# Attention gates from eight 32-column float32 products, with the tangent taken after the turn

## The reference, cut to what matters

```
h = rms_norm(x, norm1_g)
z = h @ w_in                       # 512 x 1024 by 1024 x D_IN
z_sc, z_q, z_kv, z_ng, z_ret, z_pool, z_gate = split(z)
g = sigmoid(z_ng.reshape(B, S, G, J, 3))          # the gates: 24 numbers for each position
o = g[..., 0:1] * o_cmp + g[..., 1:2] * o_slc + g[..., 2:3] * o_win
```

## Time and profile before

| what | value |
| --- | --- |
| median of 3 runs | 2067.34 us (2065.33 to 2068.14) |
| the profiled execution | 2065.34 us |
| its span, first to last instruction | 2063.5 us |
| PE busy, share of the span | 2034.1 us, 99% |
| DVE, ACT, POOL busy | 1188.9 us, 682.6 us, 916.8 us |
| mean granted PE clock | 0.996 of full speed |

### The profile page before, as it was taken

How to read it: one execution, slowest core, us unless ns; L and a number is a source line. 1 busy time by engine, 2 the same in 40 slices (tenths; PEclk the granted TensorE clock), 3 DMA queues, 4 the chain that set the end, 5 groups by cost and what they waited for, 6 DMA issues and landing times.

```text
span 2063.5 us, 31457 instructions
## 1 busy us (share of the span) xinstructions
PE 2034.1 (99%) x9836; PEld 1639.1 (79%) x9836; DVE 1188.9 (58%) x1717; ACT 682.6 (33%) x1011; POOL 916.8 (44%) x672
## 2 busy tenths in 40 slices
PE   9999999999999999999999999999999999999997
PEld 7777767888888888888887777678888888888886
DVE  7777766332327788862258667572222378888522
ACT  5365333332322222222234553333323232222222
POOL 4422333445445555555544223344444455555553
PEclk9999999999999999999999999999999999999998
DMA  5311222222223223223233113223222223222233
GB/s 211 108 52 43 77 87 88 94 100 93 98 94 102 92 92 102 92 95 112 95 126 95 53 42 96 84 82 102 92 99 94 96 87 102 93 100 97 99 104 109
DMA packets 57429, 194.87 MB, mean 94 GB/s; under 512 B 7040, under 2 KB 7552, under 8 KB 57216
## 3 DMA queue, kind: packets, MB, share of 16 engines
q1 hardware_dynamic: 52576, 186.17, 27.0%
q10 hardware_dynamic: 4768, 7.61, 1.4%
HBM read 186.67 MB, written 2.10 MB: 91 GB/s over the span
## 4 chain that ended last, share of the span: by engine, by line
PE 93%; DVE 4%; ACT 1%; issue 1%; DMA 0%; SPq 0%; DVEq 0%; ACTq 0%
PE acc L1220 28%; PE acc L1222 28%; PE acc L1221 28%; PE o L1435 2%; PE s L1405 2%; PE t L1416 2%; PE o L1475 1%; PE s L1465 1%; PE s L1313 0%; DVE pool_early L1064 0%; DMA w_raw<-weights_dram 0%; DVE sc L1058 0%; PE s L1491 0%; PE t L1456 0%; ACT pr L569 0%
## 5 line engine op out<-in xcount | busy, mean ns | idle before, releaser
L435 POOL TENSOR_TENSOR w_lo<-w_raw,w_hi 128x512 fp32r<-128x512 f32 x668 | 916.6, 1394 | 1123.2 <-ACT w_hi L457 1107.7
L1220 PE MATMUL acc<-xg_hi,w_hi 128*128 128x512 f32 x1904 | 768.7, 404 | 5.9 <-DVE sc L740 2.1
L1222 PE MATMUL acc<-xg_hi,w_lo 128*128 128x512 f32 x1904 | 743.3, 390 | 0.0
L1221 PE MATMUL acc<-xg_lo,w_hi 128*128 128x512 f32 x1904 | 742.6, 390 | 0.0
L457 ACT ACTIVATE w_hi<-w_raw 128x1024 fp32r<-128x1024 f32 x336 | 355.4, 1058 | 813.0 <-PE acc L1222 785.0
L1220 PEld LDWEIGHTS acc<-xg_hi,w_hi 128*128 128x128 f32 x1904 | 357.9, 188 | 113.8 <-issue 37.7
L1221 PEld LDWEIGHTS acc<-xg_lo,w_hi 128*128 128x128 f32 x1904 | 358.2, 188 | 77.0 <-issue 6.4
L1222 PEld LDWEIGHTS acc<-xg_hi,w_lo 128*128 128x128 f32 x1904 | 357.8, 188 | 76.2
L1097 DVE TENSOR_TENSOR work<-acc,rstd 128x512 f32<-128x512 f32 x64 | 44.1, 690 | 256.2 <-PE acc L1222 256.2
L1220 PE MATMUL acc<-act_hi,w_hi 128*128 128x512 f32 x352 | 136.9, 389 | 0.0
L1221 PE MATMUL acc<-act_lo,w_hi 128*128 128x512 f32 x352 | 136.9, 389 | 0.0
(11 more groups left out here) (208 smaller groups left out, 2206.6 us busy)
## 6 DMA issues: line engine op xcount, KB each, us to landing
w_raw<-weights_dram SPq DMA_DIRECT2D x339, 512.0 KB, 3.3
x<-xT_dram SPq DMA_DIRECT2D x8, 256.0 KB, 5.5
rot<-rq ACTq DMA_DIRECT2D x16, 128.0 KB
rot<-rk ACTq DMA_DIRECT2D x16, 128.0 KB
dec<-decay_dram ACTq DMA_DIRECT2D x8, 256.0 KB, 3.6
out_dram<-x SPq DMA_DIRECT2D x8, 256.0 KB, 2.6
con<-consts_dram SPq DMA_DIRECT2D x1, 1406.0 KB, 10.5
w1k<-w_dram SPq DMA_DIRECT2D x2, 512.0 KB, 8.7
```

Of the source, the lines that this page charges most:

```text
L435: nc.gpsimd.tensor_tensor(w_lo[:, slot, part], w_raw[:, slot, part], w_hi[:, slot, part].bitcast(F32), ALU.subtract).then_inc(lo_ready, 1)
L1220: mm(tile, w_h, right_hi, start=first, stop=False)
L1221: mm(tile, w_h, right_lo, start=False, stop=False)
L1222: return mm(tile, w_l, right_hi, start=False, stop=last)
```

## The change

The gate tile is no longer made of the split weights and the split, scaled input. DVE adds `w_hi` and `w_lo` of the 32 columns that matter back to one float32 matrix and multiplies it by the gain `norm1` (`gate_w`, 128 x 8 x 32, two instructions). PE then makes eight plain float32 matmuls of 32 weight columns with `x` itself: chunks 0 to 3 go to column groups 0 to 3 (partitions 0 to 31, 32 to 63 and so on of the bank), chunks 4 to 7 to the same four again. The bank so holds four partial sums. `take(10)` is as before. The turn is now four float32 matmuls with `fold`, a 128x32 matrix of four stacked identities, which sums the four parts while it turns. `fold` is made anew in each layer by a reduction of `ident` on DVE, ahead of `take(10)`. ACT takes the tangent from the turned bank (128x96) in SIDE's slot 2, and DVE ends the sigmoid in place. The loading and splitting of groups 10 and 11 stay.

```diff
+        gate_w = at("gate_w", [P, CH, 32], F32, R)
+        fold = small[:, 0:32]
...
-                    if g == 11:
-                        act.wait_ge(acc_free, 1 + L * TILES + 12)
-                        nc.scalar.activation(sc[:, 2, :], sc[:, 2, :], ACT.Tanh, scale=0.5).then_inc(a_made, 1)
...
+                            if e[0] == "gate":
+                                act.wait_ge(s_done, s_use(L, e))
+                                nc.scalar.activation(gates[:, :, :], s_of(e)[:, :].rearrange("p (k n) -> p k n", k=QT)[:, :, 0:3 * HEADS],
+                                                     ACT.Tanh, scale=0.5).then_inc(a_made, 1)
...
                 s_end(ins, "vc")
+                g = A_TILES.index("gate")
+                dve.wait_ge(lo_ready, 1 + 2 * (L * GROUPS + (g + 1)))
+                halves_of = [w[:, g % RING, :].rearrange("p (c n) -> p c n", c=CH)[:, :, 0:32].bitcast(F32) for w in (w_hi, w_lo)]
+                then(ve.tensor_tensor(gate_w[:, :, :], halves_of[0], halves_of[1], ALU.add))
+                v_end(ve.tensor_tensor(gate_w[:, :, :], gate_w[:, :, :], V("norm1", 0, DC).unsqueeze(2).to_broadcast([P, DC, 32]), ALU.mult), "gate_w")
                 take(9, qT[:, 3, :])
...
                 then(ve.tensor_tensor(kc[:, 0:NCMP], kc[:, 0:NCMP], C("cos_c", NCMP), ALU.mult))
+                then(ve.tensor_reduce(fold, ident.rearrange("p (j i) -> p i j", j=4), AX.X, ALU.add))
                 take(10, sc[:, 2, :])
...
                 def gate(e):
-                    s_wait(e)
-                    s_end(ve.tensor_scalar(gates[:, :, :], s_of(e)[:, :].rearrange("p (k n) -> p k n", k=QT)[:, :, 0:3 * HEADS],
-                                           1.0, 0.5, ALU.add, ALU.mult), e, wait=True)
+                    dve.wait_ge(a_made, a_count(L, "gate"))
+                    s_end(ve.tensor_scalar(gates[:, :, :], gates[:, :, :], 1.0, 0.5, ALU.add, ALU.mult), e, wait=True)
...
+                    if name == "gate":
+                        pe.wait_ge(v_made, v_count(L, "gate_w"))
+                        alone(pe)
+                        for c in range(DC):
+                            rows = slice(32 * (c % 4), 32 * (c % 4) + 32)
+                            ins = mm(acc[g % 2][rows, :], gate_w[:, c, :], x[:, c, :], start=c < 4, stop=c >= 4)
+                        ins.then_inc(halves, 4)
...
                 def gate(e):
-                    pe.wait_ge(a_made, a_count(L, "gate"))
+                    pe.wait_ge(acc_free, 1 + L * TILES + 12)
                     b = s_begin(e)
-                    alone(pe)
+                    last_wait()
                     for k in range(QT):
-                        ins = nc.tensor.transpose(b[:, k * P:k * P + 32], sc[0:32, 2, k * P:(k + 1) * P], ident[0:32, 0:32])
+                        ins = mm(b[:, k * P:k * P + 32], sc[:, 2, k * P:(k + 1) * P], fold, start=True, stop=True)
```

More of the change, by code:

```diff
@@ L149 @@
 assert len(S_USES) % 2 == 0 and len(T_USES) % 2 == 0
-V_MADE = ["win_k", "k0_scaled", "k1_scaled", "win_v", "k0", "k1", "arg", "hid", "q0", "q1", "q2", "q3", "kc", "center"]
+V_MADE = ["win_k", "k0_scaled", "k1_scaled", "win_v", "k0", "k1", "arg", "hid", "q0", "q1", "gate_w", "q2", "q3", "kc", "center"]
 A_MADE = ["hid", "gate"]
@@ L557, in _ @@
                         for e in SIDE[n]:
-                            if e[0] == "cmp_scores":
+                            if e[0] == "gate":
+                                act.wait_ge(s_done, s_use(L, e))
+                                nc.scalar.activation(gates[:, :, :], s_of(e)[:, :].rearrange("p (k n) -> p k n", k=QT)[:, :, 0:3 * HEADS],
+                                                     ACT.Tanh, scale=0.5).then_inc(a_made, 1)
+                            elif e[0] == "cmp_scores":
                                 act.wait_ge(v_made, v_count(L, e))
@@ L1247, in tile_free, with quarter @@
                     pe.wait_ge(acc_free, 1 + v)
-                def quarter(g, q, tile, wait=False, loop=None, per=0, done=1):
+                def quarter(g, q, tile, wait=False, loop=None, per=0):
                     if q == 2:
@@ L1257, in quarter, with projection @@
                     if q % 2:
-                        ins.then_inc(halves, done if q == 3 else 1)
-                def projection(g, tile, wait=False, norm=None, loop=None, per=0, done=1):
+                        ins.then_inc(halves, 1)
+                def projection(g, tile, wait=False, norm=None, loop=None, per=0):
                     for q in range(4):
-                        quarter(g, q, tile, wait, loop, per, done)
+                        quarter(g, q, tile, wait, loop, per)
                         if norm and q == norm[2]:
@@ L1326, in _ @@
                 for g, name in enumerate(A_TILES):
+                    if name not in ("gate", "pad"):
+                        group_here(g)
                     if name != "pad":
-                        group_here(g)
                         tile_free(g)
-                    if name != "pad":
+                    if name == "gate":
[5 more added lines that the diff above has]
+                        ins.then_inc(halves, 4)
+                    elif name != "pad":
                         projection(g, acc[g % 2], wait=1 if g == 0 else False,
                                    norm=("sumsq1", L * 16 + DC, 3, sum_squares) if g == 2 else
-                                   ("spread1", L * 2 + 1, 1, spread_root) if g == 3 else None,
-                                   done=3 if A_TILES[g + 1] == "pad" else 1)
+                                   ("spread1", L * 2 + 1, 1, spread_root) if g == 3 else None)
                     if g == 6:
@@ L1581, in _ @@
             ins.then_inc(spread_ready, 1)
-CHAIN_LAYER, CHAIN_J, CHAIN_F, CHAIN_D = 165, 4, 15, 2
+CHAIN_LAYER, CHAIN_J, CHAIN_F, CHAIN_D = 167, 4, 15, 2
 def _constants():
```

## The result

| | before | changed |
|---|---|---|
| median of 8 runs each | 2067.64 us | 2075.06 us (2070.67 to 2077.53) |
| profiled execution, span | 2065.34, 2063.5 us | 2077.08, 2075.3 us |
| mean granted clock over the span | 0.996 | 0.991 |

The changed kernel takes 1.0035 times as long (95% interval 1.0026 to 1.0044). It is slower, by 7.4 us; the forecast was 5.6 us, 2072.9 us. Eight products took the place of 24, PE has less to do, and the kernel lost time. The eight runs of the changed kernel differ in their clock: the fastest, 2070.67 us, has a mean granted clock of 0.994, the slowest, 2077.53 us, one of 0.990.

A forecast was written before the change was run, and what follows sets the result against it. PE held 93% of the chain of waits, but DVE's path to `take(10)` set the floor. Late start 1.35, clock 1.4 and turn 0.3 us, twice, less 0.5, made 5.6 us: 2072.9 us, range 2067.0 to 2077.5.

The forecast's parts named there:

- rival A: The forecast: DVE's chain to `take(10)` ends last, the clock falls in both layers; 2072.9 us (2070.5 to 2076), chance 0.46.
- F: PE's saving is kept: `take(10)` follows the gate products, group 12 starts 2.9 us early; 2062.1 us, chance 0.06.
- E: The gate products' column groups don't overlap, group 12 starts 1.7 us late; 2071.0 us, chance 0.07.
- B: Same DVE chain, but the clock stays, or falls while PE stands still anyway; 2070.1 us, chance 0.22.
- rival C: More DVE steps, the reduction too, stand behind POOL, and the clock costs its full 1.7 us; 2075.8 us, chance 0.11.
- Term 1: PE's gate products: 24 matmuls of some 5.4 us become eight taking 2.0 us, saving 3.4 us in each layer.
- Term 2: DVE's two new instructions ahead of `take(9)`: 0.9 us with the gap, `take(9)` 0.6 us late (0.5 to 0.8).
- Term 3: DVE's rotation of q2: two instructions stand behind POOL's halves, the next runs free; the delay stays 0.6 us.
- Term 4: POOL's group 13 starts earlier, so DVE's small keys' step L876 waits about 1.1 us (nothing to 1.27).
- Term 5: The `fold` reduction on DVE ahead of `take(10)`: 0.3 us, upper end 1.1 us more.
- Term 6: PE's clock falls to half behind a 5.1 us stop before group 12: 1.4 us, bounds 0 and 2.1.
- Term 7: The gates' turn on PE with the narrower moving side: 0.3 us more, bounds -0.1 and 0.45.

The follow-up runs named there:

- PE's part alone: The changed kernel without DVE's three new instructions, gate products taking columns of x as weights (gates not the reference's): 2074.10 us, ratio 1.0032.
- the first kernel with an early take: The changed kernel with gate weights by ACT, `fold` made early, `take(10)` right behind `take(9)`, attention steps four slots later: 2068.02 us, ratio 0.9995.
- DVE's part alone: The kernel before plus DVE's three new instructions in their places, results unused: 2068.56 us, ratio 1.0009.
- the control with 24 products: The kernel before with its 24 gate products into the idle bank `t_bank[1]` and later slots for turn and attention: 2065.24 us, ratio 0.9989.

## Why the prediction was right, point by point

- **The mechanism** (rival A): right. DVE's chain sets `take(10)`, and everything that PE saved turned into waiting. The kernel with PE's part alone and those that take the wait away show it from both sides. F, the saving kept, needed `take(10)` out of its place, as the prediction said. E is refuted by the span of 1.92 us, B by the 5.80 us of work at the half clock, D by the step of 1.24 us. By its number alone rival C, 2075.8 us, lies nearer to the measured 2075.06 than A's 2072.9. It took two things more than A: the reduction behind POOL, which did not happen (0.37 us), and a larger price of the clock, which did. So the rows decide for A's chain, and the clock's price was nearer to C's and above that too.
- **Term 1**: 2.0 us forecast, 1.92 measured. The 5.4 us of the 24 products stand, though the subtraction given for them, 5.69 less 0.46, is 5.2: 24 starts 0.227 us apart are 5.4.
- **Term 2**: 0.9 us, and `take(9)` 0.6 late. Measured 0.42 + 0.43 us and gaps; from `vcz`'s start to the take 2.18 us against 1.42, 0.76 late, inside the bounds.
- **Term 3**: right in kind. L788 took 1.45, L790 1.75, and L792 0.69 us with POOL at rest. A slip ahead of it changes nothing: L787 ended 0.42 us after POOL's first half, by the prediction's own numbers, and not 0.55. That a take, with one input in PSUM, doesn't wait for POOL was said from two rows with POOL at rest; `take(10)` now shows it, 0.69 us at 80.39 inside POOL's run.
- **Term 4**: forecast 1.1 us more; measured 1.24 less 0.19, 1.05 us more. POOL's group 13 started 5.70 us behind the small key product in place of 7.01, 1.3 us earlier where some 1.5 was said. The Trainium skill (SBUF — State Buffer, "SBUF: two separate sides") has the shared port pair locked for a whole instruction; the step grows from 0.19 to 1.24 us when POOL begins 0.07 us ahead of it, and shrinks to 0.19 when group 13 is held back, which agrees.
- **Term 5**: 0.3 us, measured 0.37, with POOL's run on at the time, so the upper end, 1.1 us more, is excluded. The Trainium skill (VectorE: DVE Perf Modes, "The perf-mode tier table") gives tensor_reduce the plain mode only; that it didn't wait for POOL agrees.
- **Group 12**: forecast 1.35 us late, measured 1.65. The 0.3 is several small things: 0.15 in term 2, 0.07 in the reduction, gaps.
- **Term 6, the one that was mis-sized**: forecast 1.4 us per layer with bounds 0 and 2.1; the profiled run shows 2.9. I took one row, 3.7 us at 0.54 behind a stop of 3.7 us, as the length of every low stretch. Behind this stop it was 6.83 us, and only 1.0 us of it fell into the stop. The kernel that fills the stop gets 2.6 us per layer back. Other kernels show 3.41 and 6.83 at this same place, one kernel shows none behind a stop of 3.64 us near 1296, so the 2.9 is not fixed either: 6.83 and 3.41 in the run with group 13 held back, 3.41 and 6.83 with ACT making the gate weights.
- **Term 7**: forecast 0.3, measured 0.45 us, its upper bound.
- **The 0.5 us in one layer**: 0.3 us in layer 0 and 1.1 in layer 1.

With the measured terms the sum is 2 x (1.65 + 2.9 + 0.45) - 1.4 = 8.6 us for the profiled pair. The medians lie 7.4 apart, which fits low stretches that are shorter in part of the runs. The clocks of the runs point that way: by their lengths one more low stretch of 3.41 us lowers the mean granted clock by 0.0008 and costs up to 1.7 us, and from 0.994 to 0.990 the runs of the changed kernel go from 2070.67 to 2077.53 us. Where in those runs the stretches lie, no profile shows. That the total, 5.6 us, came as near to 7.4 as it did is in part luck, since its clock term was half of what the profiled run shows. What the prediction didn't see is how close the good version was: it found no room for F in DVE's rows and stopped there, where one bank or one moved take, with the queue behind it in order, makes it true.

## What to carry to other kernels

Before work is taken off the busiest engine, look who gives the buffer back that its next step needs: if that engine has only tenths of a microsecond of slack there, as DVE had, the saving becomes a stop, and more can be lost behind it: here PE came back at half clock, which cost 2.9 us in each layer of the profiled run. Ask also what the earlier end sets off: here it started POOL's next split just ahead of a 0.19 us step of DVE. Then the place to change is the buffer (another bank, an earlier take, a count given earlier) together with the queue behind it; here the fewer products paid only after that.

## What the runs showed of the hardware

- Float32 products whose weights have 32 columns run on four column groups side by side, with all 128 rows and 512 moving columns: 16 passes in 1.92 us, where one after another they would be some 6.4 us (an estimate from eight passes of 128 columns in 0.80 us).
- At the gates and near 281 and 1305 us the clock's low level came while PE stood still or within 2 us of its start, and lasted 3.41 or 6.83 us; the same kernel shows either at the same place of its two layers. Behind the stops of 4.2 us and more at the gates, every profiled layer had it; behind 2.0 us at group 13 (the first kernel with an early take) both layers, behind 2.33 us one of two, behind 1.5 us (DVE's part alone) none. Behind the stops of 3.64 to 3.73 us ahead of the product of `pr` and `rv`, it came in 27 of the 28 layers profiled, and not in layer 1 of the control with 24 products. In every kernel the clock was also low in the last 8 us or more, where PE has little to do (before: 0.51 from 2052.80 to 2063.50).
- An instruction of 31 columns on DVE with both inputs in SBUF took 0.19 us with POOL at rest and 1.05 to 1.27 us beside it; a reduction of 128 columns, with one input, took 0.37 to 0.39 us beside it and 0.38 without.
